# A transformer block on one core: the units of its first stage in another order

## The reference

```
xn = rmsnorm(x);  p = xn @ w_in                    # attention q, k, v; recurrence pb; gates pg
o_a = attention(q, k, v)                           # 8 heads of 64, causal, bias by distance
pb_mix = pb + mu * (shift(pb) - pb)                # each column mixed with the token before
r, k, v, xw, xa, xg = split(pb_mix)
decay = exp(-exp(-softplus(-(w0 + tanh(xw) @ Wup)) - 0.5));  a = sigmoid(a0 + xa @ Aup);  g = sigmoid(xg) @ Gup
kk = k * k_k / |k * k_k|                           # norm over a head's 64 columns
state = state * decay - (state kk)(kk a)^T + v k^T;  o = state r      # over 256 tokens
o_b = (groupnorm(o) * lnx_g + lnx_b + (r . k r_k) v) * g
y = sigmoid(pg_a) * (o_a @ w_proj_a) + sigmoid(pg_b) * (o_b @ w_proj_b);  h = x + y @ w_out
out = rmsnorm(h + peer_ffn(rmsnorm(h)))            # 8 x 16 of 16384 experts
```

## Time and profile before

| | us |
|---|---|
| median of 3 runs (lowest, highest) | 1153.72 (1153.16, 1154.04) |
| the profiled execution | 1152.36 |
| its span in the profile | 1150.3 |
| PE busy | 1095.0 |
| DVE, ACT, POOL busy | 761.1, 601.3, 459.0 |
| mean granted clock of TensorE | 0.981 |

### The profile page before, as it was taken

How to read it: one execution, slowest core, us unless ns; L and a number is a source line. 1 busy time by engine, 2 the same in 40 slices (tenths; PEclk the granted TensorE clock), 3 DMA queues, 4 the chain that set the end, 5 groups by cost and what they waited for, 6 DMA issues and landing times.

```text
span 1150.3 us, 23537 instructions
## 1 busy us (share of the span) xinstructions
PE 1095.0 (95%) x7802; PEld 1011.3 (88%) x7804; DVE 761.1 (66%) x1473; ACT 601.3 (52%) x1097; POOL 459.0 (40%) x215
## 2 busy tenths in 40 slices
PE   6989769999999999999999999999999999999997
PEld 5986749999999999989999999998888888888885
DVE  4475686424462899994588888886555555555554
ACT  4445544224545544445577777775544545454453
POOL 1064343336711799897877676761000000000000
PEclk8997989999999999999999999999999999999999
DMA  5652211124555445545544444444555555555553
GB/s 212 237 168 71 89 40 56 38 74 147 182 185 166 146 166 169 179 162 167 184 162 149 161 150 160 151 159 147 195 189 199 186 197 192 191 197 188 199 186 124
DMA packets 51985, 181.71 MB, mean 158 GB/s; under 512 B 5795, under 2 KB 7843, under 8 KB 51820
## 3 DMA queue, kind: packets, MB, share of 16 engines
q1 hardware_dynamic: 51948, 181.21, 46.3%
HBM read 180.13 MB, written 1.06 MB: 158 GB/s over the span
## 4 chain that ended last, share of the span: by engine, by line
PE 74%; issue 9%; POOL 8%; DVE 5%; ACT 1%; DMA 1%; another core or an unknown queue 0%; POOLq 0%; SPq 0%; DVEq 0%; ACTq 0%
PE PS L379 12%; PE PS L380 11%; PE PS L381 11%; PE PS L756 10%; PE PS L755 10%; PE PS L754 10%; POOL lo L995 8%; PE PS L702 1%; PE PS L703 1%; DVE arena L1103 1%; PE PS L566 1%; PE PS L571 1%; DVE arena L1188 1%; PE PS L553 1%; DVE arena L1139 1%
## 5 line engine op out<-in xcount | busy, mean ns | idle before, releaser
L995 POOL TENSOR_TENSOR lo<-raw,hi 128x1024 fp32r<-128x1024 f32 x172 | 438.3, 2555 | 247.8 <-ACT hi L768 247.6
L768 ACT CAST hi<-raw 128x1024 fp32r<-128x1024 f32 x332 | 347.1, 1046 | 178.6 <-DMA raw<-in_v_units 170.8
L379 PE MATMUL PS<-xh,hi 128*128 128x256 f32 x1440 | 417.9, 290 | 11.3 <-POOL lo L995 6.8
L380 PE MATMUL PS<-xl,hi 128*128 128x256 f32 x1440 | 409.2, 284 | 0.0
L381 PE MATMUL PS<-xh,lo 128*128 128x256 f32 x1440 | 409.0, 284 | 0.0
L1057 DVE TENSOR_TENSOR lo<-raw,hi 128x1024 fp32r<-128x1024 f32 x160 | 195.7, 1225 | 179.0 <-ACT hi L768 179.0
L379 PEld LDWEIGHTS PS<-xh,hi 128*128 128x128 f32 x1440 | 277.9, 193 | 16.2 <-POOL lo L995 8.4
L380 PEld LDWEIGHTS PS<-xl,hi 128*128 128x128 f32 x1440 | 278.2, 193 | 0.0
L381 PEld LDWEIGHTS PS<-xh,lo 128*128 128x128 f32 x1440 | 277.9, 193 | 0.0
L754 PE MATMUL PS<-hi,xh 128*128 128x512 f32 x512 | 199.3, 389 | 0.0
L756 PE MATMUL PS<-lo,xh 128*128 128x512 f32 x512 | 199.2, 389 | 0.0
(11 more groups left out here) (264 smaller groups left out, 1166.6 us busy)
## 6 DMA issues: line engine op xcount, KB each, us to landing
raw<-in_u_units SPq DMA_DIRECT2D x128, 512.0 KB, 3.2
raw<-in_v_units SPq DMA_DIRECT2D x128, 512.0 KB, 3.2
raw<-in_w_in_units SPq DMA_DIRECT2D x44, 512.0 KB, 3.3
raw<-in_w_q_units SPq DMA_DIRECT2D x16, 512.0 KB, 3.3
raw<-in_w_proj_units SPq DMA_DIRECT2D x8, 512.0 KB, 3.2
raw<-in_w_out_units SPq DMA_DIRECT2D x8, 512.0 KB, 3.3
arena<-in_x SPq DMA_DIRECT2D x2, 512.0 KB, 4.8
arena<-bias_rows SPq DMA_DIRECT2D x2, 512.0 KB, 4.5
```

What stands on the lines that cost most here:

```text
L379: mm(ps, hi[:, s, c], mh[:, k, :], start=(k == k0), stop=False)
L380: mm(ps, hi[:, s, c], ml[:, k, :], start=False, stop=False)
L768: nc.scalar.copy(hi[:, j, :], raw[:, j, :]).then_inc(hi_made, 1)
L995: nc.gpsimd.tensor_tensor(lo[:, j, :], raw[:, j, :], hi[:, j, :].bitcast(F32), ALU.subtract).then_inc(lo_pool, 1)
```

## The change

The weights are laid out in another order, and so the units of the first stage are done in another one, 43 instead of 44:

- units 0 to 14 are the inputs of the recurrence (decay and rate inputs first, then k, the gate input, r, v), 15 to 26 q, k, v of attention, 27 to 42 the gates.
- The mix is made unit by unit and out of PSUM: ACT writes (1 - mu) times the product (`mix_evac`), DVE adds mu times the product of the token before (`mix_in`). Units 0 to 14 use three PSUM banks, and PE waits for the mix of product g - 3 before product g.
- DVE makes the low parts of units 0 to 3 only, POOL those from 4 on.
- The low-rank products, the key norm and the matrices are placed between units; the attention scores and softmax come after the matrices. POOL's part of the preparation of the inversion moves to DVE.
- The sums over heads of the key norm and of the group norm are now taken with a full 128 x 128 block matrix, four products of 256 columns, whose result already stands in every column. So `spread_heads` goes, and square root and reciprocal work on full width: 1024 columns for the key norm (line 1166), two times 512 for the group norm (line 1299). The mean is subtracted by a centring matrix in the product.
- Gate units 27 to 30 and 39 to 42 are only copied, and their sigmoid is taken later over four units at once (line 920 for the last four).
- The projections use four banks and run in halves: the first (attention) halves of k = 0 to 2, then by turns the second half of k and the first half of k + 3. `unit_done` is incremented by the second half.
- All slots are counted by (unit number) mod 4, since the number of units is no multiple of 4 any more.

The mixes, which free PE's banks, stand between the steps of the key norm. The diff, cut to its core:

```diff
...
+U_QKV = NMIX
+U_GATE = U_QKV + 3 * CT
+ACT_IN = 3 * CT + NB_GATE
+LO_FIRST = 4
...
+        def unit_bank(g):
+            return g % 3 if g < NMIX else g % 2
...
+            def in_unit(g, tile_ready=None):
+                splits_ready(g, *((lo_dve, g + 1) if g < LO_FIRST else (lo_pool, g + 1 - LO_FIRST)))
+
+                before = [p for p in range(g) if unit_bank(p) == unit_bank(g)]
+                if before and before[-1] < NMIX:
+                    pe.wait_ge(mix_made, before[-1] + 1)
+                elif before:
+                    pe.wait_ge(act_evac, 2 + before[-1] - NMIX + 1)
+                product(PS[:, unit_bank(g), 0:T], g % 4, xh, xl, tile_ready=tile_ready).then_inc(unit_done, 1)
...
-            for g in range(U_PROJ, U_OUT):
-                k = g - U_PROJ
-                splits_ready(g, lo_pool, g + 1 - NB_R)
-                if k >= 3:
-                    pe.wait_ge(y_made, k - 2)
-                product(PS[:, PROJ_BANKS[k % 3], 0:T], g % 4, oh, ol, 0, 4)
-                if k == 0:
-                    pe.wait_ge(ob_made, 1)
-                product(PS[:, PROJ_BANKS[k % 3], T:2 * T], g % 4, oh, ol, 4, 8).then_inc(unit_done, 1)
...
+            def projection(k, half):
+                g = U_PROJ + k
+                if half == 0:
+                    splits_ready(g, lo_pool, g + 1 - LO_FIRST)
+                    if k == 2:
+                        pe.wait_ge(act_evac, 2 + evacs)
+                    if k >= 4:
+                        pe.wait_ge(y_made, k - 3)
+                elif k == 0:
+                    pe.wait_ge(ob_made, 2)
+                return product(PS[:, PROJ_BANKS[k % 4], T * half:T * half + T], g % 4, oh, ol, 4 * half, 4 * half + 4)
+
+            for k in range(3):
+                projection(k, 0)
+            for k in range(KT):
+                projection(k, 1).then_inc(unit_done, 1)
+                if k + 3 < KT:
+                    projection(k + 3, 0)
...
+            def mix_evac(*gs):
+                for g in gs:
+                    nc.scalar.activation(mix[g], finished(g), ACT.Copy, scale=vec[:, V_KEEP + g:V_KEEP + g + 1]
+                                         ).then_inc(mix_half, 1)
...
+            gate_copy(40)
+            output_high(0)
+            gate_copy(41)
+            output_high(1)
+            gate_copy(42)
...
             for g in range(U_PROJ, U_OUT):
                 k = g - U_PROJ
-                next_hi(g // 4, g % 4)
+                hi_ahead(g, 0, 0)
                 act.wait_ge(ysum_made, k + 1)
-                nc.scalar.copy(xh[:, k, :], PS[:, PROJ_BANKS[k % 3], 0:T]).then_inc(yh_made, 1)
+                nc.scalar.copy(xh[:, k, :], PS[:, PROJ_BANKS[k % 4], 0:T]).then_inc(yh_made, 1)
...
+            def mix_in(*gs):
+
+                for g in gs:
+                    dve.wait_ge(mix_half, g + 1)
+                    V.scalar_tensor_tensor(out=mix[g][:, 1:T], in0=PS[:, unit_bank(g), 0:T - 1], scalar=per_channel(V_MU + g),
+                                           in1=mix[g][:, 1:T], op0=ALU.mult, op1=ALU.add).then_inc(mix_made, 1)
...
+            mix_in(10)
+            link(V.reciprocal(tmp, tmp))
+            link(V.tensor_tensor(kk, kk, tmp, ALU.mult))
+            mix_in(11)
...
+            for b in range(2):
+                dve.wait_ge(osq_made, b + 1)
+                last = V.tensor_tensor(half_bank(b), half_bank(b), gB[:, 2 * b:2 * b + 2, :], ALU.mult)
...
+            for b in range(2):
+                dve.wait_ge(gn_root, b + 1)
+                last = V.reciprocal(rstd[:, 2 * b:2 * b + 2, :], rstd[:, 2 * b:2 * b + 2, :])
...
-PROJ_BANKS = [0, 1, 7]
+PROJ_BANKS = [6, 7, 0, 1]
```

More of the change, by code:

```diff
@@ L104, in block_program @@
         ident = con[:, C_ID:C_ID + P]
[L105 removed]
+        centred = con[:, C_CEN:C_CEN + P]
+        one = con[:, C_M4 + T - 1:C_M4 + T]
         blk = con[:, C_BLK:C_BLK + P]
@@ L317, in _ @@
                     sp.dma_start(Sb[:, h0:h0 + 4, P * qt:P * qt + P + P * qt], src).then_inc(bias_in, 16)
-            with sp.Fori(5, U_PROJ // 4) as i:
-                for j in range(RAW):
-                    sp.wait_ge(unit_done, 4 * i + (j - 3))
-                    load(w_in[4 * i + j], j)
             for g in range(U_PROJ, U_OUT):
@@ new lines, in _, with head_sums @@
+                b = 3 + 2 * (c // 2)
+                mm(PS[:, b, o], lwa[0:LORA, col], mixw[0:LORA, 0, :], start=True, stop=True)
+                last = mm(PS[:, b + 1, o], lwa[LORA:P, col], mixw[LORA:P, 0, :], start=True, stop=True)
+                if c % 2:
+                    last.then_inc(lor_ps, 1)
+            units(5, 6)
+            def head_sums(banks, stationary, src, done):
+                for c in range(CT):
+                    last = mm(PS[:, banks[c // 2], T * (c % 2):T * (c % 2) + T], stationary, src[:, c, :], start=True,
+                              stop=True)
+                    if c % 2:
+                        last.then_inc(done, 1)
@@ L502, in _ @@
-            units(28, 29, 30, 31)
+            for c in range(CT):
+                col, o = slice(P * c, P * c + P), slice(T * (c % 2), T * (c % 2) + T)
+                mm(PS[:, 4 + c // 2, o], lg0[:, col], mixg[:, 0, :], start=True, stop=False)
+                last = mm(PS[:, 4 + c // 2, o], lg1[0:32, col], mixg[0:32, 1, :], start=False, stop=True)
+                if c % 2:
+                    last.then_inc(g_lor_ps, 1)
+            units(*range(9, 19))
             pe.wait_ge(rkv_made, 1)
-            pe.wait_ge(vA_sb, 2)
+            pe.wait_ge(lor_g, 2)
@@ L667, in _ @@
             for t in range(NT):
-                last = mm(PS[:, 7, t:t + 1], gt[:, P * t:P * t + P], ones[:, 0:1], start=True, stop=True)
+                last = mm(PS[:, 7, t:t + 1], gt[:, P * t:P * t + P], one, start=True, stop=True)
             last.then_inc(ss_made, 1)
@@ L801, in gate_evac, with gate_copy @@
                 for g in gs:
[L802 to L807 removed]
+                    nc.scalar.activation(gates[:, gate_row(g), :], finished(g), ACT.Sigmoid).then_inc(act_evac, 1)
+            def gate_copy(*gs):
+                for g in gs:
+                    nc.scalar.copy(gates[:, gate_row(g), :], finished(g)).then_inc(act_evac, 1)
@@ new lines, in _ @@
+            for c2 in range(2):
+                act.wait_ge(lor_ps, c2 + 1)
+                for dst, v0, b in ((lw, V_W0, 3), (aB, V_A0, 4)):
+                    for c in (2 * c2, 2 * c2 + 1):
+                        nc.scalar.activation(dst[:, c, :], PS[:, b + 2 * c2, T * (c % 2):T * (c % 2) + T], ACT.Sigmoid,
+                                             bias=vec[:, v0 + c:v0 + c + 1]).then_inc(lor_sb, 1)
+            mix_evac(5, 6)
+            act.wait_ge(mix_made, 7)
+            nc.scalar.activation(mixg[:, 0, :], mixg[:, 0, :], ACT.Sigmoid).then_inc(lor_act, 1)
```

667 lines of the change are left out of this document (309 added, 358 removed).

## The result

The changed kernel takes 1184.95 us (median of 4 runs, 1183.51 to 1185.37) beside 1153.44 us (4 runs) for the kernel before: ratio 1.0272, 95% interval 1.0254 to 1.0290, 31.5 us slower. The forecast was 1181, range 1166 to 1198. The profiled execution took 1185.37 us, its span is 1183.6 (before: 1150.3).

What follows compares the result with a forecast made beforehand. TensorE was taken as the bound, busy 1095.0 of 1150.3 us. Ahead of the projections -11.3, in them +38.5, together +27.2: span 1177.5, and with what runs add to the span 1181 us, range 1166 to 1198.

Steps and rivals of the forecast that it cites:

- The loop in the projections: Projections: first half k+3 waits for sum, copy, cast and low part; five periods of 9.8 us, 38.5 with both ends.
- the 2.5 us at the output units: End of the projections: the first output unit waits, its cast standing behind a sum; adds 2.5 us.
- the two neighbouring workings: Projection period worked out at full clock (8.2 us) and at 0.21 us a matmul (10.4), each with 0.2 for signals.
- The upper bound of the loop: Projections: at most 37.5 us for the five products, beside 1.5 and 2.5 for the two ends.
- Low-rank products: Before the key norm: small products and two units take 11.2 us against 22.6, without wait at full clock; saves 11.4.
- Key norm on DVE: Early mixes: 1024-column reciprocal and GpSimd blocking make PE wait before products 13 to 16; adds 9.5 us, bounds 3 and 15.
- Softmax: Wait before the probability transposes: about 20.5 us behind four units of 11.5, wait 9 against 8.3; adds 1 us.
- Entry: Before the first projection: group norm reciprocals, then cast and low part; wait 5.9 us against 0.9, adds 5.
- Front in all: Everything ahead of the projections: 26.8 us taken away, 9.5, 1 and 5 added, net -11.3.
- The loop ran at full clock: Rival for the projections: no low clock behind the waits, 34.5 becomes 26.5; about 1171 us, chance 0.13.
- The early part: Rival ahead of the projections: GpSimd and DVE block each other more often, terms at upper bounds; about 1193 us, chance 0.17.
- The faster rival: Projections: the loop does not close if the fourth unit's cast precedes the first sum's copy; about 1139 us, chance 0.06.

Runs made afterwards that it cites:

- filler experiment: The changed kernel with 40 useless matmuls into an unused PSUM bank ahead of each of the five waiting first halves: 1173.98 us.
- recip_quarter: The changed kernel with the key norm's reciprocal taken of 256 of 1024 columns, a constant for the other 768: 1182.68 us.
- lows_vector_quarter: The changed kernel with low parts of units 4 to 15 on DVE and the key norm's reciprocal of 256 columns, constant elsewhere: 1181.10 us.

## Why the prediction held, and where it was off

*The loop in the projections* was right in mechanism, and its size was set low: 38.5 forecast, 42.6 measured. The chain was right (5.06 read from the earlier trace rows, 5.09 measured; five waits of 5.27, 5.12, 5.13, 5.13, 5.13), and so was the 2.5 us at the output units (2.28). The mis-sized term is the clock. I let 15 of the 24 matmuls behind each wait run at 0.21 us, from the 3 us at 0.50 in the earlier trace rows. All of the first 5 us ran at a granted 0.50, 23 matmuls in 5.0 us. So a period was 10.5 and not 9.8, the head (48 matmuls behind the entry wait) took 8.6 instead of 5.8, and the tail 8.0. Over the 192 matmuls the clock cost 15.0 us (38.0 of work between waits instead of 23.0), where I had 8.5. The other way, I had put 0.4 us into each period for signals, where the two neighbouring workings have 0.2; the five waits measured 5.16 on average and not 5.5. The upper bound of the loop, 37.5 + 4, still lay below the 42.6.

*Low-rank products*: 11.2 forecast (5.4 + 5.8), 12.8 measured (7.0 + 5.8). Two records make one product; the 8 products of decay and rate, in pairs beside each other, take 2.0 us, and the 8 of the gate input 5.0:

```profile
34.02 0.48 PE L439 MATMUL PS<-arena 64*128 64x256 f32 x1
...
35.64 0.38 PE L440 MATMUL PS<-arena 64*128 64x256 f32 x1
...
49.27 0.60 PE L462 MATMUL PS<-arena 128*128 128x256 f32 x2
...
53.56 0.69 PE L463 MATMUL PS<-arena 32*128 32x256 f32 x2
```

That is 0.62 us for each of the latter, at full clock, where I had 0.45 from another product (L626). The term was mis-sized by 1.6; why they take longer, no run shows. No wait before them, as forecast.

*Key norm on DVE*: 9.5 forecast, 9.7 measured, the step right by its sum more than by its parts. The reciprocal (6.5) and the blocking were there, but it was the blocking that set the end: I took 4.8 + 2.4 of it, 1.7 + 4.2 stand in the five steps L1169 and L1172, and 2.9 us less in DVE's queue ahead of them let product 15 start only 0.6 us earlier. The place was also another, one long wait where one or two of 2 to 7 us were named: products 13 to 16 were named, with a wait of g for the mix of g - 3, but product 14 waits only 0.8 us for the mix of 11, and nearly all of it stands before product 15, the first that uses two banks by turns and so needs the mix of 13, not of 12. Not in the sum was the low clock behind it: 97 matmuls in 14.3 us at a granted 0.79, against 11.5 at full clock, 2.8 us.

*Softmax*: 8.3 to 8.9, +0.6 (forecast +1). *Entry*: 5.45 us, forecast 5.9. *Front in all*: -9.6 measured, -11.3 forecast. The low-rank products (1.6) and the low clock (2.8) account for the difference and more; about 2 us of gain that stand against them were not traced.

*Rivals.* The loop ran at full clock only in the filler experiment (1174). The early part gave back little more than was counted. The faster rival named the cast's place as the deciding point; moved there, the kernel took 1159.95 and not 1139, since the slot was a second such point that I had not seen, and the bank a third.

*The sum.* A loop 4.1 us dearer, a front 1.7 us poorer and 0.3 behind them make a span 6.1 longer than forecast (1183.6 against 1177.5). The median lies 1.35 above the span, where I had added 3.5. 6.1 - 2.1 = 4.0, from 1181 to 1184.95. That the last step hid a third of the error is luck.

## What to carry to other kernels

When an order puts a piece of work ahead of the step that frees its own inputs, write down the cycle: who makes each input, what stands ahead of it in that engine's queue, and which of these wait for the piece just done; if it closes, its period is the sum of all the engines in it, however little each is busy, and opening it at one queue helps only until the next resource (here the slot, and with it the bank) closes it again. Price a wait of some 5 us together with the work at half clock behind it: 2.2 us on each here. And before moving work between DVE and GpSimd, look which instructions it will stand beside, not only how long it takes.

## What the runs showed of the hardware

- Useless matmuls in a wait of 5 us made the kernel 11 us faster (granted clock 1.00 instead of 0.50 in the work behind it).
- GpSimd's subtraction of 128x1024 stretches a DVE multiplication of two SBUF operands of 128x1024 from 1.21 to 2.89 us, four smaller steps from 1.67 to 5.85 or 7.98 us, and leaves a reciprocal (6.54 in both) and the mix with one operand in PSUM (0.48 in both) alone.
- A DVE instruction with one input can be stretched too: the TENSOR_SCALAR of 128x768 in recip_quarter took 2.00 us beside GpSimd's row, and 0.55 in lows_vector_quarter, where GpSimd stood still.
- In recip_quarter six subtractions by GpSimd in a row took 16.75 us, 2.8 each, against 2.40 by themselves: the blocking also costs GpSimd something.
